# Value products of two heads side by side in two attentions, and a new order of the rounds in the selected-key attention

## The reference, cut to what matters

```python
# dilated: per group g, head h
s = q @ k.T * scale + band;  p = exp(s - max);  o_g = (p / sum(p)) @ v_g;  o = sum_g weight_g * o_g
# selected keys: per head h
o = gate0 * softmax(q kc + mask) @ vc + gate1 * softmax(q ks + causal) @ vs + gate2 * softmax(q kw + causal) @ vw
```

## Time and profile before

| what | us |
|---|---|
| median of 3 runs (lowest, highest) | 4246.82 (4241.04, 4247.91) |
| the profiled execution | 4245.55 |
| its span, first to last instruction | 4243.8 |
| dilated attention, first half, roughly | 645 to 745 |
| dilated attention, second half, roughly | 972 to 1075 |
| selected-key attention, roughly | 2038 to 2241 |
| mean granted TensorE clock | 0.973 of full |

### The profile page before, as it was taken

One profiled execution on the slowest core, in us unless ns is written; L12 is line 12 of the kernel. 1 busy time (PEld: TensorE's weight loads), 2 busy tenths in 40 slices (PEclk: granted clock), 3 DMA queues, 4 the chain that ended last, 5 costly groups with the idle time before them and its releaser, 6 DMA issues. The chain is left out here.

```text
span 4243.8 us, 54933 instructions
## 1 busy us (share of the span) xinstructions
PE 4012.8 (95%) x19521; PEld 3372.3 (79%) x19521; DVE 2635.1 (62%) x4865; ACT 1622.5 (38%) x2364; POOL 534.0 (13%) x549
## 2 busy tenths in 40 slices
PE   7999998998999989999899999999999999999998
PEld 6887776776788878887677888757889999988886
DVE  6632766576465256524773332585998788688887
ACT  3222235335322133223683221453335555533333
POOL 1100000000010001000100000000004455233332
PEclk9999999999999989999899999989999999999999
DMA  7632320320364226523002222202338989899997
GB/s 280 228 119 94 115 84 6 114 79 31 141 232 158 99 95 230 189 95 108 6 1 97 92 99 99 88 4 98 125 115 285 341 324 350 310 337 353 354 353 277
DMA packets 140165, 700.59 MB, mean 165 GB/s; under 512 B 18375, under 2 KB 19750, under 8 KB 94638
## 3 DMA queue, kind: packets, MB, share of 16 engines
q1 hardware_dynamic: 66574, 423.83, 27.9%
q0 software_dynamic: 73440, 274.76, 17.6%
HBM read 635.55 MB, written 59.80 MB: 164 GB/s over the span
## 5 line engine op out<-in xcount | busy, mean ns | idle before, releaser
L112 DVE TENSOR_TENSOR w_lo<-raw,w_hi 128x2048 fp32r<-128x2048 f32 x331 | 758.6, 2292 | 711.4 <-ACT w_hi L104 707.0
L124 PE MATMUL ps<-x_hi,w_hi 128*128 128x512 f32 (+1 forms) x2896 | 1092.5, 377 | 60.0 <-DVE w_lo L112 36.1
L125 PE MATMUL ps<-x_lo,w_hi 128*128 128x512 f32 (+1 forms) x2896 | 1078.2, 372 | 0.0
L126 PE MATMUL ps<-x_hi,w_lo 128*128 128x512 f32 (+1 forms) x2896 | 1077.8, 372 | 0.0
L104 ACT ACTIVATE w_hi<-raw 128x2048 fp32r<-128x2048 f32 x331 | 632.6, 1911 | 666.8 <-PE ps L126 422.1
L124 PEld LDWEIGHTS ps<-x_hi,w_hi 128*128 128x128 f32 x2896 | 549.0, 190 | 148.0 <-issue 54.7
L126 PEld LDWEIGHTS ps<-x_hi,w_lo 128*128 128x128 f32 x2896 | 548.0, 189 | 75.3
L125 PEld LDWEIGHTS ps<-x_lo,w_hi 128*128 128x128 f32 x2896 | 549.2, 190 | 73.2
L2340 POOL DMA_INDIRECT ph_rows<-in_peer_u,ph_names x128 | 222.2, 1736 | 1281.2 <-DVE ph_names L2710 1017.4
L2423 PE MATMUL ps<-w_hi,px_gh 128*128 128x512 f32 x768 | 300.2, 391 | 4.7 <-DVE px_gl L2763 4.7
L2423 PE MATMUL ps<-w_lo,px_gh 128*128 128x512 f32 x768 | 300.0, 391 | 0.0
(11 more groups left out here) (404 smaller groups left out, 5637.5 us busy)
## 6 DMA issues: line engine op xcount, KB each, us to landing
raw<-in_slabs SPq DMA_DIRECT2D x331, 1024.0 KB, 4.9
ada_ring<-in_w_ada POOLq DMA_DIRECT2D x160, 512.0 KB, 5.3
act_dram<-px_act SPq DMA_DIRECT2D x64, 384.0 KB, 7.4
gate_dram<-ps_g SPq DMA_DIRECT2D x12, 2048.0 KB, 12.7
px_g<-gate_dram POOLq DMA_DIRECT2D x32, 768.0 KB, 8.2
px_ai<-act_dram POOLq DMA_DIRECT2D x64, 384.0 KB, 6.5
h_dram<-h SPq DMA_DIRECT2D x2, 2048.0 KB, 8.0
h<-h_dram SPq DMA_DIRECT2D x2, 2048.0 KB, 8.4
```

The costliest lines, as they stand in the source:

```text
L112: nc.vector.tensor_tensor(k.wlo[:, c % 2, :], k.raw[:, c % 2, :], k.whi[:, c % 2, :].bitcast(F32), ALU.subtract).then_inc(k.raw_free, 1)
L124: mm(out, hi, rhs_hi, start=start, stop=False)
L125: mm(out, hi, rhs_lo, start=False, stop=False)
L126: return mm(out, lo, rhs_hi, start=False, stop=stop)
```

## The change

In both attentions the stationary operand of a value product becomes the 64 value columns of one head, the output goes to that head's 64 rows, and the products of the two heads are issued by turns. The count of products is the same.

Dilated: both heads write bank 6 + p % 2 (`out`), so pairs alternate between the banks; `values(u)` waits for all copies of the round, and for `o` only of the pair before the last; `high` and `low` are one instruction of 128 rows per pair; `low` stands behind both `scaled`.

Selected keys: the order of items becomes head 2p branch 0, head 2p + 1 branch 0, head 2p branch 1, head 2p + 1 branch 1. Odd items are multiplied together with the one before: chunk 0 in the odd round, chunks 1 and 2 in the even round behind it. `scores_c` moves to the end of round 2, `shifted_c` into round 3 behind two of the scalings, `exps_c` to the end of round 3, `scaled_c` to round 0, `values_c` to round 3, `out_high` to the start of round 1, `staged` to odd rounds. The semaphore `pv` is split in three, one for each chunk. The items' and slots' numbering (`item`, `item_c`, POOL's wait) follows.

```diff
@@ -757,24 +758,31 @@
...
-            def values(u, h2):
+            def out(p, h2):
+                return k.ps[rows(h2), (6 + p % 2) * T:(7 + p % 2) * T]
+
+            def values(u):
                 p, rq = divmod(u, NB)
-                v = 2 * u + h2
-                pe.wait_ge(s["copied"], 3 * v + 3)
-                if rq == 0 and p:
-                    pe.wait_ge(s["o"], 2 * p - 1 + h2)
+                pe.wait_ge(s["copied"], 6 * u + 6)
+                if rq == 0 and p > 1:
+                    pe.wait_ge(s["o"], p - 1)
                 for g in (1, 2):
-                    last = nc.tensor.matmul(bank(k, 6 + h2, P, rq * P), vt[:, g, rq, p * P:(p + 1) * P],
-                                            pt1[:, u % 2, h2, (g - 1) * P:g * P], start=rq == 0 and g == 1, stop=False)
-                last.then_inc(s["pv"], 1)
-
-            def values0(p, h2):
-                out = bank(k, 6 + h2).rearrange("p (r m) -> p r m", r=NB)
+                    for h2 in range(2):
+                        last = nc.tensor.matmul(out(p, h2)[:, rq * P:(rq + 1) * P],
+                                                vt[:, g, rq, p * P + HD * h2:p * P + HD * (h2 + 1)],
+                                                pt1[:, u % 2, h2, (g - 1) * P:g * P], start=rq == 0 and g == 1, stop=False)
+                        if g == 2:
+                            last.then_inc(s["pv"], 1)
+
+            def values0(p):
                 for i in range(NB):
                     at = min(32 * i, HD)
-                    last = nc.tensor.matmul(out[:, :, at:at + HD], vt[:, 0, i, p * P:(p + 1) * P],
-                                            pt0[:, h2, i, :, :], start=False, stop=i == NB - 1)
-                last.then_inc(s["pv0"], 1)
+                    for h2 in range(2):
+                        last = nc.tensor.matmul(out(p, h2).rearrange("p (r m) -> p r m", r=NB)[:, :, at:at + HD],
+                                                vt[:, 0, i, p * P + HD * h2:p * P + HD * (h2 + 1)],
+                                                pt0[:, h2, i, :, :], start=False, stop=i == NB - 1)
+                        if i == NB - 1:
+                            last.then_inc(s["pv0"], 1)
@@ -785,10 +793,9 @@
...
-                for h2 in range(2):
-                    values(u, h2)
-                    if u % NB == NB - 1:
-                        values0(u // NB, h2)
+                values(u)
+                if u % NB == NB - 1:
+                    values0(u // NB)
@@ -813,9 +820,9 @@
...
-            def high(p, h2):
-                act.wait_ge(s["pv0"], 2 * p + h2 + 1)
-                A(out_hi(p)[rows(h2)], k.ps[rows(h2), (6 + h2) * T:(7 + h2) * T], ACT.Copy).then_inc(s["high"], 1)
+            def high(p):
+                act.wait_ge(s["pv0"], 2 * p + 2)
+                A(out_hi(p), bank(k, 6 + p % 2), ACT.Copy).then_inc(s["high"], 1)
@@ -823,11 +830,10 @@
...
-                    if u % NB == 0 and u:
-                        high(u // NB - 1, h2)
+                    if u % NB == 0 and u and h2 == 0:
+                        high(u // NB - 1)
                     copies(u, h2)
-            for h2 in range(2):
-                high(U // NB - 1, h2)
+            high(U // NB - 1)
@@ -862,10 +868,9 @@
...
-            def low(p, h2):
-                ve.wait_ge(s["high"], 2 * p + h2 + 1)
-                V.tensor_tensor(out_lo(p)[rows(h2)], k.ps[rows(h2), (6 + h2) * T:(7 + h2) * T],
-                                out_hi(p)[rows(h2)].bitcast(F32), ALU.subtract).then_inc(s["o"], 1)
+            def low(p):
+                ve.wait_ge(s["high"], p + 1)
+                V.tensor_tensor(out_lo(p), bank(k, 6 + p % 2), out_hi(p).bitcast(F32), ALU.subtract).then_inc(s["o"], 1)
@@ -877,12 +882,11 @@
...
                 for h2 in range(2):
-                    if u % NB == 0 and u:
-                        low(u // NB - 1, h2)
                     if u + 1 < U:
                         scaled(u + 1, h2)
-            for h2 in range(2):
-                low(U // NB - 1, h2)
+                if u % NB == 0 and u:
+                    low(u // NB - 1)
+            low(U // NB - 1)
@@ -1384,12 +1389,12 @@
...
         def head(g):
-            return g // 2, g % 2
+            return 2 * (g // 4) + g % 2, g % 4 // 2
@@ -1397,10 +1402,10 @@
...
         def item(g, b):
-            return 17 * (g // 4) + 4 * (g % 4) + b + (g % 4 > 1)
+            return 17 * (g // 4) + 4 * (g % 4) + b + (g % 4 > 2)

         def item_c(p):
-            return 17 * p + 8
@@ -1431,7 +1436,7 @@
...
                 if h >= 4:
-                    gp.wait_ge(s["s"], item(2 * (h - 4) + 1, 3) + 1)
+                    gp.wait_ge(s["s"], item(4 * ((h - 4) // 2) + 2 + h % 2, 3) + 1)
                     gp.wait_ge(s["s"], item_c((h - 4) // 2) + 1)
@@ -1488,51 +1493,54 @@
...
             def values(g, c):
-                h, i = head(g)
-                p = h // 2
-                if g % 4 == 0 and c == 0 and p > 1:
+
+                p = g // 4
+                if g % 4 == 1 and c == 0 and p > 1:
                     pe.wait_ge(s["o"], p - 1)
                 pe.wait_ge(s["copied"], chunk(g, c) + 1)
                 for kb, at in CHUNKS[c]:
-                    v = (64 if h % 2 == 0 else 0) + P * (8 * i + 2 * kb + h // 8)
                     n = (NB - kb) * P
-                    last = nc.tensor.matmul(bank(k, 6 + p % 2, n, kb * P), vz[:, v:v + P], pt_at(g, c, at, n),
-                                            start=g % 4 == 0 and c == 0, stop=g % 4 == 3 and c == 2)
-                if c == 2:
-                    last.then_inc(s["pv"], 1)
+                    for of in (g - 1, g):
+                        h, i = head(of)
+                        v = HD + P * (8 * i + 2 * kb + h // 8)
+                        to = (6 + p % 2) * T + kb * P
+                        last = nc.tensor.matmul(k.ps[HD * (h % 2):HD * (h % 2) + HD, to:to + n], vz[:, v:v + HD],
+                                                pt_at(of, c, at, n), start=i == 0 and c == 0, stop=i == 1 and c == 2)
+                last.then_inc(s[("pv0", "pv1", "pv2")[c]], 1)
...
-            for g in range(-4, G):
-                ahead, now, turned = g + 4 < G, g >= 0, 0 <= g + 1 < G
+            for g in range(-4, G + 1):
+                ahead, now, turned = g + 4 < G, 0 <= g < G, 0 <= g + 1 < G
+                odd, even = now and g % 2, g > 1 and g % 2 == 0
                 if ahead:
                     scores(g + 4, 0)
-                if now:
-                    values(g, 0)
+                if g % 4 == 3 and now:
+                    values_c(g // 4)
+                if even:
+                    values(g - 1, 1)
                 if ahead:
                     scores(g + 4, 1)
                 if turned:
                     turn(g + 1, 0)
                 if ahead:
                     scores(g + 4, 2)
-                if now:
-                    values(g, 1)
+                if odd:
+                    values(g, 0)
+                if even:
+                    values(g - 1, 2)
                 if turned:
                     turn(g + 1, 1)
                 if ahead:
                     scores(g + 4, 3)
-                if now:
-                    values(g, 2)
                 if turned:
                     turn(g + 1, 2)
                 if g % 4 == 1 and now:
                     turn_c(g // 4)
-                if g % 4 == 2 and now:
-                    values_c(g // 4)
-                if g % 4 == 1 and ahead:
+                if g % 4 == 2 and ahead:
                     scores_c((g + 4) // 4)
@@ -1561,8 +1569,8 @@
...
-                    act.wait_ge(s["pv"], g - 2)
+                if g > 2:
+                    act.wait_ge(s[("pv0", "pv1", "pv2")[c]], (g - 3) // 2 + 1)
@@ -1573,11 +1581,12 @@
...
             def out_high(p):
-                act.wait_ge(s["pv"], 4 * p + 4)
+                act.wait_ge(s["pvc"], p + 1)
+                act.wait_ge(s["pv2"], 2 * p + 2)
                 A(k.xh[:, p, :], bank(k, 6 + p % 2), ACT.Copy).then_inc(s["xh"], 1)

             for g in range(-4, G):
-                if g % 4 == 0 and g > 0:
+                if g % 4 == 1 and g > 1:
                     out_high(g // 4 - 1)
@@ -1591,8 +1600,8 @@
...
-                if g % 4 == 2 and g + 4 < G:
-                    exps_c((g + 4) // 4)
+                if g % 4 == 3 and g + 1 < G:
+                    exps_c((g + 1) // 4)
@@ -1682,30 +1691,35 @@
...
             for g in range(-4, G):
-                scaling, ahead = 0 <= g + 2 < G, g + 4 < G
+                scaling, ahead, compressed = 0 <= g + 2 < G, g + 4 < G, g % 4 == 3 and g + 1 < G
                 if scaling:
                     weights(g + 2)
+                if compressed:
+                    if scaling:
+                        scale(g + 2, 0)
+                        scale(g + 2, 1)
+                    shifted_c((g + 1) // 4)
                 if ahead:
                     maximum(g + 4, 0)
                     maximum(g + 4, 1)
```

(28 more changed lines are left out.)

## The result

The changed kernel took 4192.3 us, median of four runs (4190.22 to 4196.16), against 4246.41 for the kernel before beside it (four runs, 4241.04 to 4247.91). The ratio is 0.9879, 95% interval 0.9864 to 0.9895: 54 us shorter, clear of the spread of the runs, where 32.5 were forecast. The profiled execution took 4190.57, with a span of 4188.8, 55.0 less than before.

The account below looks back on a forecast made before the run. PE's chain was taken as the bound, in dilated rounds through ACT's copy, in selected keys with DVE through the score banks. Dilated 16.4 plus selected keys 16.1 gave 32.5; 4245.55 - 32.5 = 4213 us, range 4199 to 4242.

Parts of the forecast that it names:

- the overlap itself: Value products in both attentions: two half-width products on the two column halves take one product's time.
- first rival: Both attentions: column halves run one after the other; dilated +11.6, selected keys -5, total 4252 us; chance 0.09.
- second: Both attentions: array empties at every change of column half, no overlap, 0.2 us more per block; 4272 us; chance 0.05.
- The round with the long product: Dilated `values0` round: scores at 675.39 instead of 676.33, gain 0.94 us, four times per stage.
- The dilated values' loop through ACT's copy: Ordinary dilated round of 5.13 us: a loop through ACT's last copy, not PE's own work.
- third rival: Both attentions: overlap, but 0.2 us at each change into or out of column halves; 4223 us; chance 0.13.
- fifth rival: Selected keys: ACT takes DVE's place, so only 1 us gained per pair; 4222 us; chance 0.10.
- The fourth: Attention stages: granted clock falls to half once per pair, 16 times in place of 3; 4232 us; chance 0.07.
- Change: 0: Ordinary dilated round: values wait for the last copy, same work behind it, so no change from 5.13 us.
- The 1.48: Dilated round after `values0`: wait for `low` goes, round becomes ordinary, 6.61 - 5.13 = 1.48 us, three times per stage.
- 2.4: Selected keys: DVE's waiting per pair of heads falls from 3.6 to 1.2 us, gaining 2.4 us per pair.
- its loop without waits for PE is ... 20.4 us: Selected keys: DVE becomes the bound, its loop per pair 24.00 - 1.88 - 0.85 - 0.86 = 20.4 us.

Follow-up runs that it names:

- nsa_full: Changed kernel with selected-key value products 128 columns wide again, 64 of them zeros, new order kept; 4213.46 us, ratio 0.9934 to the kernel before.
- c_old: Changed kernel with the selected keys' compressed work back in its old rounds, overlap and turns of heads kept; 4207.89 us, ratio 0.9926 to the kernel before.
- by_head: Changed kernel with the dilated half-width products issued one head after the other; 4198.02 us, ratio 0.9901 to the kernel before.
- by_two: Changed kernel with the dilated long product issued by twos, two products of one head, then two of the other; 4180.21 us, one run.
- before_again: The kernel before the change, run once more with nothing edited; 4238.78 us, ratio to its own copy 1.0.
- nsa_only: The kernel before with only the selected-key half of the change; 4218.53 us, ratio 0.9961.
- one_bank: Changed kernel with all dilated pairs of heads accumulating in one bank, low still behind the scalings; 4217.29 us, one run.

## Why the prediction was wrong

**Right:** the overlap itself, complete (first rival and second fall: starts 7 ns apart; `nsa_full` shows what no overlap gives, 206.8, 2.6 us slower than before in the selected keys, where the rival had 5 us faster, though the clock has a share in that). The round with the long product, 0.99 against 0.94. The dilated values' loop through ACT's copy. The third rival's time (4223) did not come, but its rule is there in the records: I took nothing for the way into the column halves, and it costs 0.1 us (0.203 for 0.110). The Trainium skill (TensorEngine Tiling (Array Packing), Key Properties) says that a change of mode drains the array, and the rows agree for the column halves. In the dilated rounds this lay beneath PE's wait for ACT; in the selected keys no run took it away, and since DVE still waits 1.8 us a pair for PE, a part of it may be in there. The fifth rival fell: ACT is busy 91% of a pair (19.08 of 21.02), and the pair still gained 2.98 at full clock. The fourth fell as well: the clock was at half for 37.5 us of the three stages both before and after, less in the dilated ones (17.1 to 10.2), more in the selected keys (20.5 to 27.3).

**Wrong, in three places.**

First, the step "The profiled execution took 4245.55 ... 4245.55 - 32.5 = 4213". It took the 3828 us outside the stages as a constant, and with them the range. They are one draw: the same code took 3806 to 3828 in 14 profiles, and the profile that I summed against is the longest of these. This is 13.1 of the 22.5 us by which the profiled span's gain exceeded the sum, and it alone carried the time out of the range: with the stages' 41.9 it would have been 4245.55 - 41.9 = 4203.7. The medians moved as well (54.1 us between them the first time, 41.3 when both were run again), so it is not this one profile alone; whether it goes by execution, build or chip stays open.

Second, the dilated stages, 22.2 for 16.4. The term of an ordinary round, "Change: 0", was 5.13 to 5.07, over 24 such rounds 1.4 us; the long rounds add 8 x 0.05 = 0.4. Both are one thing: the first weight load behind PE's wait, which nothing hides, takes 0.133 us with 64 columns and 0.186 with 128. And 6.9 us less at half clock, at the 1.6 that 3.4 us of it cost in my rows, is worth 3.2 (an estimate; 21.4 in all, 0.8 stays unplaced). The fall behind the waits of 1.04 and 0.77 was in my rows, and I used it for the range's lower end, not for the sum. The 1.48 was right as a size and wrong as a cause, so its size was luck: I gave it to the alternating banks and to one `low` behind both scalings, and with both undone the round stays at 5.15. By elimination it came from the merging.

Third, the selected keys, 19.7 for 16.1. The mean of six distances from one pair's output to the next fell from 23.73 to 21.05 us, 16.1 together, where 6 x 2.4 = 14.4 were forecast; the two ends of the stage gave 3.6 where 2.4 - 0.7 = 1.7 were. Undisturbed, a pair went from 24.00 to 21.02, 2.98. DVE's waits went from 3.8 to 1.8 (I had 3.6 to 1.2), so this term gave 2.0 and not 2.4, and that the pair came out near its forecast is partly luck: 0.83 came from the term "its loop without waits for PE is ... 20.4 us": a wait stood inside a record, where I took it for work. DVE's line 1669 on 8 columns took 1.00 us, beside a copy by POOL (here one pair ahead of the earlier trace rows; in that pair it is the same):

```profile
2106.16 1.04 POOL L1436 CAST na_q<-nsa_qT 64x1024 fp32r<-64x1024 f32 x1 [9.77 <-PE ps L1449]
2106.23 1.00 DVE L1669 TENSOR_SCALAR na_dc<-na_dc 128x8 f32<-128x8 f32 x1
```

After, no copy by POOL stands there, and it takes:

```profile
2116.02 0.17 DVE L1678 TENSOR_SCALAR na_dc<-na_dc 128x8 f32<-128x8 f32 x1
```

Its mean of 999 ns stood in the view of lines by form, beside the earlier trace rows, and I hadn't asked why. That all of the 0.83 reached the pair's time is worked out from DVE's account of it (busy 19.26 to 18.36); no run moved the copy alone.

Of the marks that I set: PE busy below 85% of a pair was wrong (19.70 of 21.02, 94%; its records are longer, and overlapped ones count as busy), DVE 87% for 89, wait before the shift gone as expected, and the clock at half lay in four stretches of the three stages, within the five that I allowed.

## What to carry to other kernels

Two products of 64 output columns on the two column halves cost one here; issue them within four records of each other, and give the freed engine something to do (values one round later gave 29.7 us, more than the 22.2 of the whole dilated half of this change). Before adding up an engine's work, look for records far longer than their size: a wait may be inside. Sum against the stages that change, and give the rest of the span its own spread from several profiles.

## What the runs showed of the hardware

- A DVE TENSOR_SCALAR of 128x8 took 0.17 us alone and 1.00 us when POOL's copy of 64x1024 had begun 0.07 us before it; both ended within 0.04 us of each other. Before the change this was so in four of eight pairs (1.00 each); in two others the copy began behind it, in the last two none was near, and it took 0.17. In `c_old` two met a copy halfway and took 0.45 and 0.51, and in four more the copy had ended 0.28 us ahead: 0.17. The Trainium skill (SBUF — State Buffer, Who interferes with whom) says that DVE and GpSimd share a port pair which whoever issues first holds for the whole instruction, and that `tensor_scalar` is among the operations that can need it; the six records agree. No run here moved POOL's copy alone.
- Half-width products of two heads overlap even when they are not neighbours: with four records of one head ahead of the other's, the two heads' first records started 13 ns apart (128 columns, `by_head`) or 7 ns (256 columns, `by_two`). With eight ahead, the first four ran alone.
- Between full width and the two column halves the start of the next record comes some 0.09 us later than in a stream, in either direction (0.203 for 0.110 in, 0.316 for 0.216 out to the row halves). Transposes into one column half alone, among full-width ones, start after 0.109, as in a stream.
- The clock in the dilated stages, once under way, over all profiles: with one PE wait of 0.97 or 1.04 us in each round of 5.1 it stayed whole. With waits of 1.04 and 0.77 close behind each other (the kernel before, `before_again`, `nsa_only`) it fell to half behind 11 of 18 such pairs of waits, with one wait of 2.50 (`one_bank`) beside 4 of 6. At the start, PE waits 1.9 and 1.8 to 2.0 us: this brought no fall in the first stage in any of the 14 profiles, and a fall in the second in all 14. So the length of a wait alone doesn't settle it.
